# Three of the four weight sums of a Strassen group as accumulating loads instead of VectorE operations

## What is computed

```python
# block 1
h = rmsnorm(x, norm_ffn[l])
x = x + (jax.nn.silu(h @ w_gate[l]) * (h @ w_up[l])) @ w_down[l]
# block 2: a three-tap causal convolution along the tokens lies between
h2 = rmsnorm_2(x, ffn_norm_w[l])
up = causal_dwconv(h2 @ w_ffn_up[l], conv_w[l], conv_b[l])
a, b = jnp.split(up, 2, axis=-1)
x = x + (jax.nn.silu(a) * b) @ w_ffn_down[l]
```

## Time and profile before

| what | value |
|---|---|
| time, median of 3 runs | 2568.08 us (2567.1 to 2568.77) |
| profiled execution: its own time | 2568.49 us |
| its span in the trace | 2566.5 us |
| PE busy | 2531.9 us, 99% of the span, 11526 matmuls |
| DVE busy | 1851.5 us, 72% |
| ACT busy | 1300.8 us, 51% |
| POOL busy | 6.2 us |
| HBM read | 476.57 MB, 187 GB/s over the span |

### The profile page before, as it was taken

One profiled execution on the slowest core, in us unless ns is written; L12 is line 12 of the kernel. 1 busy time (PEld: TensorE's weight loads), 2 busy tenths in 40 slices (PEclk: granted clock), 3 DMA queues, 4 the chain that ended last, 5 costly groups with the idle time before them and its releaser, 6 DMA issues.

```text
span 2566.5 us, 28192 instructions
## 1 busy us (share of the span) xinstructions
PE 2531.9 (99%) x11526; PEld 2091.9 (82%) x11526; DVE 1851.5 (72%) x1646; ACT 1300.8 (51%) x1240; POOL 6.2 (0%) x15
## 2 busy tenths in 40 slices
PE   8999999999999999999999999999999999999997
PEld 7888888788888888888888888888888888888886
DVE  5565667788888888867554555555789999999996
ACT  6544555444444444455444553334565555555554
POOL 0000000000000000000000000000000000000000
PEclk9999999999999999999999999999999999999999
DMA  8455446655555555556555555556565555555551
GB/s 279 154 174 187 141 148 213 205 195 196 195 196 196 196 197 197 180 179 207 172 172 174 187 166 196 188 189 197 168 225 197 193 193 193 194 196 197 197 195 67
DMA packets 239616, 480.50 MB, mean 187 GB/s; under 512 B 7633, under 2 KB 7761, under 8 KB 239233
## 3 DMA queue, kind: packets, MB, share of 16 engines
q1 hardware_dynamic: 238496, 474.10, 55.2%
q0 software_dynamic: 992, 4.60, 0.5%
HBM read 476.57 MB, written 2.10 MB: 187 GB/s over the span
## 4 chain that ended last, share of the span: by engine, by line
PE 93%; DVE 3%; ACT 2%; issue 1%; DMA 0%; SPq 0%; DVEq 0%; ACTq 0%
PE acc L604 24%; PE acc L608 23%; PE acc L606 23%; PE misc L604 6%; PE misc L608 6%; PE misc L606 6%; PE misc L637 2%; ACT w_hi L1006 2%; DVE x L1459 1%; DVE w_lo L1431 1%; DVE hid L1791 0%; PE misc L721 0%; PE misc L701 0%; DMA x<-in_x 0%; PE misc L715 0%
## 5 line engine op out<-in xcount | busy, mean ns | idle before, releaser
L1431 DVE TENSOR_TENSOR w_lo<-w_raw,w_hi 128x2048 fp32r<-128x2048 f32 x407 | 930.6, 2290 | 361.9 <-ACT w_hi L1006 360.2
L1006 ACT ACTIVATE w_hi<-w_raw 128x2048 fp32r<-128x2048 f32 x407 | 778.8, 1916 | 501.6 <-PE acc L608 376.5
L604 PE MATMUL acc<-w_hi,xt_hi 128*128 128x512 f32 x1456 | 576.2, 396 | 0.4 <-issue 0.4
L608 PE MATMUL acc<-w_hi,xt_lo 128*128 128x512 f32 x1456 | 567.5, 390 | 0.0
L606 PE MATMUL acc<-w_lo,xt_hi 128*128 128x512 f32 x1456 | 566.7, 389 | 0.0
L604 PEld LDWEIGHTS acc<-w_hi,xt_hi 128*128 128x128 f32 x1456 | 273.6, 188 | 59.4 <-DVE x L1459 2.6
L608 PEld LDWEIGHTS acc<-w_hi,xt_lo 128*128 128x128 f32 x1456 | 273.3, 188 | 57.9
L606 PEld LDWEIGHTS acc<-w_lo,xt_hi 128*128 128x128 f32 x1456 | 273.6, 188 | 55.1
L1431 DVE TENSOR_TENSOR w_lo<-w_raw_more,w_hi 128x2048 fp32r<-128x2048 f32 x101 | 231.4, 2291 | 76.8 <-ACT w_hi L1006 76.5
L1006 ACT ACTIVATE w_hi<-w_raw_more 128x2048 fp32r<-128x2048 f32 x101 | 193.6, 1917 | 145.7 <-PE acc L608 79.4
L604 PE MATMUL misc<-w_hi,xt_hi 128*128 128x512 f32 x640 | 251.2, 393 | 3.6 <-DVE ht_lo L1437 3.6
(11 more groups left out here) (264 smaller groups left out, 3086.0 us busy)
## 6 DMA issues: line engine op xcount, KB each, us to landing
w_raw<-in_w_in SPq DMA_DIRECT2D x136, 1024.0 KB, 5.1
w_raw<-in_w_ffn_up SPq DMA_DIRECT2D x60, 1024.0 KB, 5.1
w_raw<-in_w_out SPq DMA_DIRECT2D x32, 1024.0 KB, 5.1
w_raw<-in_w_up SPq DMA_DIRECT2D x32, 1024.0 KB, 5.2
w_raw<-in_w_down SPq DMA_DIRECT2D x30, 1024.0 KB, 6.1
w_raw<-in_w_gate SPq DMA_DIRECT2D x28, 1024.0 KB, 5.2
w_raw_more<-in_w_ffn_up SPq DMA_DIRECT2D x28, 1024.0 KB, 5.0
w_raw<-in_w_ffn_down SPq DMA_DIRECT2D x28, 1024.0 KB, 7.0
```

What stands on the lines that cost most here:

```text
L604: nc.tensor.matmul(bank, hi[:, j, :], w_hi[:, t % RING, j, :], start=first and j == 0, stop=False, skip_group_check=shared)
L608: end = nc.tensor.matmul(bank, lo[:, j, :], w_hi[:, t % RING, j, :], start=False, stop=last and j == C - 1, skip_group_check=shared)
L1006: nc.scalar.activation(w_hi[:, t % RING], raw_tile(steps[t].slot), ACT.Copy).then_inc(hi_ready, 1)
L1431: nc.vector.tensor_tensor(w_lo[:, t % RING], raw_tile(steps[t].slot), w_hi[:, t % RING].bitcast(F32), ALU.subtract).then_inc(lo_ready, 1)
```

## The change

The sums for P7, P6 and P4 are no longer DVE operations. POOL issues for each a DMA that reads a weight tile from HBM and adds it to the raw slot in place (`accum_op=ALU.add`). The sum for P5 remains a DVE operation. Where the DVE operation subtracted, all four sums are now additions: T(P5) = B11 + B12, T(P7) = B12 + B22, T(P6) = T(P5) + B22, T(P4) = T(P6) + B21; the signs of the activation sums and of three result additions are turned to match. The tiles B22 and B21 are still loaded on their own for P3 and P2, so they are read from HBM twice or three times (B22 for P3, P7 and P6; B21 for P2 and P4).

POOL issues three such DMAs in each iteration, in this order: P7's after DVE's P5 sum, P6's after the `w_lo` of P5 is done, P4's after the `w_lo` of P6 is done (`lo_ready`). Each sum kind has a semaphore of its own, for which ACT waits before its `w_hi`. The slot of B22 is released once the `w_lo` of P3 is done (before: of U3, the step ahead of P7); the release of B21 comes to the same as before. The first hunk of the diff adds two blank lines only and is left out.

```diff
--- before.py
+++ after.py
@@ -111,7 +113,7 @@
 
 Load = namedtuple("Load", "weight row col slot release")
 Step = namedtuple("Step", "slot count")
-Sum = namedtuple("Sum", "count slot other other_count")
+Sum = namedtuple("Sum", "kind count slot other other_count weight row col ready")
 
 
 def plan_weights():
@@ -148,8 +150,8 @@
                  "G2": (a_weight, 2 * N, a_col), "G3": (a_weight, 3 * N, a_col),
                  "U2": (b_weight, 2 * N, b_col), "U3": (b_weight, 3 * N, b_col)}
         where.update({f"D{n}": (up_weight, (i - 1) * N, n * N) for n in range(Q)})
-        release = {"B11": at["P4"], "B12": at["P7"], "B22": max(at["P3"], at["P6"] - 1, at["P7"] - 1),
-                   "B21": max(at["P2"], at["P4"] - 1)}
+        release = {"B11": at["P4"], "B12": at["P7"], "B22": at["P3"],
+                   "B21": at["P2"]}
         here = {}
 
         def need(name):
@@ -159,8 +161,14 @@
 
         for name in order:
             if name in T_FORMS:
-                mine, other = need(T_FORMS[name][0]), need(T_FORMS[name][1])
-                sums[at[name]] = Sum(len(sums) + 1, mine.slot, other.slot, other.count)
+                mine = need(T_FORMS[name][0])
+                chunk = len(sums) // 4 + 1
+                if name == "P5":
+                    other = need("B12")
+                    sums[at[name]] = Sum(name, chunk, mine.slot, other.slot, other.count, None, None, None, None)
+                else:
+                    ready = {"P6": at["P5"], "P4": at["P6"], "P7": None}[name]
+                    sums[at[name]] = Sum(name, 16 * chunk, mine.slot, None, None, *where[T_FORMS[name][1]], ready)
                 steps.append(Step(mine.slot, None))
             else:
                 steps.append(need(RAW_FORMS.get(name, name)))
@@ -490,7 +498,7 @@
     dve_link = sem("dve_link")
 
     hid_ready = sem("hid_ready")
-    sum_ready = sem("weight_sum_ready")
+    sum_ready = {"P5": sem("t1_ready"), "P6": sem("t2_ready"), "P7": sem("t3_ready"), "P4": sem("t4_ready")}
     s_sum_ready = sem("s_sum_ready")
     s_hi_done = sem("s_hi_done")
     s_lo_done = sem("s_lo_done")
@@ -583,13 +591,28 @@
         load(mult_a[:], ins["mult_a"], tables_loaded)
         load(taps[:], ins["taps"], tables_loaded)
 
+        def weight_sums(ffn, i):
+
+            for name in ("P7", "P6", "P4"):
+                sm = sums[iteration_t(ffn, i) + order_of(ffn, i).index(name)]
+                if name == "P7":
+                    pool.wait_ge(sum_ready["P5"], nth(ffn, i))
+                else:
+                    pool.wait_ge(lo_ready, sm.ready + 1)
+                pool.dma_start(raw_tile(sm.slot), tile_of(ins[sm.weight][0], sm.row, sm.col),
+                               accum_op=ALU.add).then_inc(sum_ready[name], 16)
+
         pool.wait_ge(tile_used, FFN1_T + 1)
         load(final_row[:], ins["norm_final"].partition_broadcast(P), row_loaded)
+        for i in range(1, NF):
+            weight_sums(1, i)
         pool.wait_ge(lo_ready, more_free[1] + 1)
         load(decay[:], ins["decay"], tables2_loaded)
         load(rope_r[:], ins["rope_r"], tables2_loaded)
         load(causal[:], ins["causal"], tables2_loaded)
 
+        for i in range(1, NF):
+            weight_sums(2, i)
         pool.wait_ge(tile_used, iteration_t(2, NF - 1) + order_of(2, NF - 1).index("P4") + 1)
         load(final_row[:], ins["final_norm_w_2"].partition_broadcast(P), row_loaded)
 
@@ -998,7 +1021,7 @@
             if t >= STEPS:
                 return
             if t in sums:
-                act.wait_ge(sum_ready, sums[t].count)
+                act.wait_ge(sum_ready[sums[t].kind], sums[t].count)
             else:
                 act.wait_ge(raw_ready[steps[t].slot], steps[t].count)
             if t >= RING:
@@ -1413,16 +1436,16 @@
             links[0] += 1
             dve.wait_ge(dve_link, links[0])
 
-        def weight_sum(t):
+        def t1_sum(t):
 
             dve.wait_ge(raw_ready[sums[t].other], sums[t].other_count)
             mine = raw_tile(sums[t].slot)
-            nc.vector.tensor_tensor(mine, raw_tile(sums[t].other), mine, ALU.subtract).then_inc(sum_ready, 1)
+            nc.vector.tensor_tensor(mine, mine, raw_tile(sums[t].other), ALU.add).then_inc(sum_ready["P5"], 1)
 
         def split(t):
 
-            if t + 1 in sums:
-                weight_sum(t + 1)
+            if t + 1 in sums and sums[t + 1].kind == "P5":
+                t1_sum(t + 1)
             if t >= STEPS:
                 return
             if t not in sums:
@@ -1743,10 +1766,10 @@
                                          ALU.add))
             a11, a12, a21, a22 = (a_sum[:, k * C:(k + 1) * C, tok * P:(tok + 1) * P]
                                   for tok in range(TOK) for k in range(2))
+            link(nc.vector.tensor_tensor(s_sum[:, 0], a21, a22, ALU.subtract))
+            link(nc.vector.tensor_tensor(s_sum[:, 1], s_sum[:, 0], a11, ALU.subtract))
             nc.vector.tensor_tensor(s_sum[:, 2], a11, a21, ALU.subtract)
-            link(nc.vector.tensor_tensor(s_sum[:, 0], a21, a22, ALU.add))
-            link(nc.vector.tensor_tensor(s_sum[:, 1], s_sum[:, 0], a11, ALU.subtract))
-            nc.vector.tensor_tensor(s_sum[:, 3], a12, s_sum[:, 1], ALU.subtract).then_inc(s_sum_ready, 1)
+            nc.vector.tensor_tensor(s_sum[:, 3], a12, s_sum[:, 1], ALU.add).then_inc(s_sum_ready, 1)
 
         def s_lo_piece(ffn, lo, hi):
             dve.wait_ge(s_hi_done, ffn)
@@ -1758,23 +1781,23 @@
             scale = rstd[:, 1 if ffn == 1 else 4, :]
             key = (f"sums{ffn}", i)
 
-            def plus(dst, bank, tok):
+            def plus(dst, bank, tok, op=ALU.add):
                 return nc.vector.scalar_tensor_tensor(out=dst, in0=bank, scalar=scale[:, tok:tok + 1], in1=dst,
-                                                      op0=ALU.mult, op1=ALU.add)
+                                                      op0=ALU.mult, op1=op)
 
             if name == "P6":
                 dve.wait_ge(p5_copied, n)
                 dve.wait_ge(tile_used, t + 1)
-                plus(dst_b[:, 0, :], acc[:, 0, 0, :], 0).then_inc(p6_added, 1)
+                plus(dst_b[:, 0, :], acc[:, 0, 0, :], 0, ALU.subtract).then_inc(p6_added, 1)
             if name == "U3":
                 dve.wait_ge(p6_added, n)
                 dve.wait_ge(tile_used, t + 1)
-                plus(dst_b[:, 0, :], misc[:, 2, :], 0).then_inc(drained[2], 1)
+                plus(dst_b[:, 0, :], misc[:, 2, :], 0, ALU.subtract).then_inc(drained[2], 1)
             if name == "P7":
                 dve.wait_ge(p7_copied, n)
                 dve.wait_ge(tile_used, t + 1)
                 nc.vector.scalar_tensor_tensor(out=dst_b[:, 1, :], in0=acc[:, 0, 1, :], scalar=scale[:, 1:2],
-                                               in1=dst_a[:, 1, :], op0=ALU.mult, op1=ALU.add).then_inc(pair_read[0], 1)
+                                               in1=dst_a[:, 1, :], op0=ALU.mult, op1=ALU.subtract).then_inc(pair_read[0], 1)
             if name == "P2":
                 dve.wait_ge(p1_copied, n)
                 dve.wait_ge(tile_used, t + 1)
```

## The result

The changed kernel takes 2662.98 us (median of 4, 2659.81 to 2667.53), the kernel before on the same chip 2567.59 us (2565.57 to 2568.77). The ratio is 1.0378, with a 95% interval of 1.0365 to 1.0391: 95 us slower. The forecast was 2599 us, with a range up to 2650. (One of the four executions of e7 further down took 12046 us, for a reason that no run shows; its median counts that one, its ratio leaves it out.)

A forecast was written before the change was run, and what follows sets the result against it. The prediction took TensorE (PE) to bound the kernel nearly everywhere: nine second-stage stalls of 3.4 us, 31 us, on the profiled 2568.5 us gave 2599.5, less 0.4 for the median: 2599 us, range 2565 to 2650.

The forecast's parts named there:

- PE bounds the kernel, and the removed sums hide behind it: Whole kernel: PE busy 2531.9 of 2566.5 us; removing 60 sums, 137 us of DVE time, priced at nothing for PE.
- Throughput is no bound, only the latency of P6's DMA counts: Added DMAs: three add at most 15.6 us to 37.6 us of 64.8 per iteration; P6's has the least room.
- The free time is 7.9 us in the second stage and 10.8 in the first: Longest X before PE waits ahead of U2: 7.9 us in the second feed-forward stage, 10.8 in the first.
- X: Time from the end of P5's `w_lo` to P6's sum being ready; forecast 11.4 us in the second stage.
- X = 11.4 us: Second stage: P6's DMA queues behind P7's, shares with G3's and B21's loads, and lands at 2217.3, counted from 2205.94.
- 5.2 us in the sum: Engine time of one accumulating 1 MB DMA, taken as twice a plain load's 2.6 us.
- The factor of 1.5 for sharing: Accumulating DMA beside plain loads gets two thirds of the engines, so P6's 5.2 us become 7.8 us.
- the start of 1.9 us: Time from a DMA's issue to its first data, taken as about 1.9 us from plain loads.
- In the first stage it fits by 0.1 us: First stage: P6's sum lands at 738.9 against a limit of 738.8, 0.1 us, counted as nothing.
- The fall of the clock is left out of the forecast: Lower PE clock behind each second-stage stall: 15 to 21 us in nine iterations, kept only in the range.
- The sum was 31 us: Total forecast loss: PE idle 3.4 us ahead of U2 in nine second-stage iterations, nothing in the first stage.
- 6 us of stall, with a fallen clock: Second stage: the case that set the range's upper end, 2650 us.

The follow-up runs named there:

- e7: Changed kernel with the old release of B22's slot, at U3's `w_lo`, so G3's, B21's and D0's loads come later again: 2586.80 us, ratio 1.0074.
- e6: Changed kernel with P6's DMA issued ahead of P7's and ACT's copy of P5's result ahead of P6's `w_hi`: 2568.47 us, ratio 1.0002.
- e1: Changed kernel with P6's sum back on DVE; P7's and P4's stay accumulating DMAs: 2568.91 us, ratio 1.0005.
- e2: Changed kernel with POOL issuing P6's DMA ahead of P7's: 2578.94 us, ratio 1.0044.
- e4: Changed kernel with P6's DMA a plain copy without the addition, so P6 and P4 products differ from the reference: 2586.85 us, ratio 1.0072.
- e8: Changed kernel with P7's sum back on DVE and the old release of B22 that it needs: 2584.00 us, ratio 1.0069.

## Why the prediction was wrong

- *PE bounds the kernel, and the removed sums hide behind it*: right. e6 measures it: ratio 1.0002 with all of them gone.
- *Throughput is no bound, only the latency of P6's DMA counts*: right (e1, and e6 with all 60 DMAs).
- *The free time is 7.9 us in the second stage and 10.8 in the first*: right. The prediction counts X from the end of P5's `w_lo`, 0.3 us ahead of the issue. Counted so, the means less 7.9 give stalls of 5.8, 1.3, 1.9, 1.8 and 1.7 us, where 5.8, 1.4, 1.9, 1.9 and 1.8 were measured (changed kernel, e2, e4, e7, e8). The first stage has 13.1 - 10.8 = 2.3, measured 2.5.
- *X = 11.4 us*: this step failed; counted the same way 13.7 were measured in the mean and 13.9 in the iteration above. There, P6's packets were to begin 3.0 us after `w_lo` and began after 4.9, they were to take 7.8 us and took 8.7, and the landing took 0.3 instead of 0.6. The term that was too small is the time of one accumulating DMA's packets: 5.2 us in the sum, 6.0 us for the one alone (e2). It counts twice, since P7's DMA is drawn out by it too (7.4 us instead of 6.7). The 5.2 are twice a load at "some 400 GB/s", while the row named beside it, 329 GB/s at a share of 0.90, makes 366 GB/s at full share and twice 2.9 us. The rest of the late start is 0.8 us between P7's last packet and P6's first, in which G3's load moves alone; the sum has nothing there, and why it is so no run shows. The factor of 1.5 for sharing was about right (8.7 / 6.0 = 1.45), and so was the start of 1.9 us (2.0).
- The prediction overlooked that a third load, D0's, moves into the same stretch. The trace gives no sign that it counts: the other queue moves 131 GB/s beside P6's DMA whatever stands in it, and at that rate B21's load alone would last about 8 us (an estimate), past the end of P6's. No run takes D0's load away by itself.
- *In the first stage it fits by 0.1 us*: failed with the same X, 13.1 us instead of 10.9. The stall is 2.5 us nine times, 22 us.
- *The fall of the clock is left out of the forecast*: failed. The rows shown pointed at it for waits of 3.3 us and more; at 5.8 us it falls in every iteration (behind the shorter stalls of the first stage in three of nine), and over both stages it costs about 25 us, a quarter of the loss.
- The sum was 31 us and became 52 + 22 + 25 = 99 us in the profiled execution (95 us between the medians). The mechanism, the place and the count (nine, ahead of U2) were as written; of the 68 us too few, 2.3 us in one latency made 21 (second stage) and 22 (first stage), and the clock 25.

The range reached to 2650 us for "6 us of stall, with a fallen clock" in the second stage, and forgot that an X that long stalls the first stage as well.

The Trainium skill's rule that an add in the DMA path costs two source reads and runs at half the rate of a copy ("Collectives: The Full Stack", the bandwidth ceiling) agrees with this case: 207 GB/s against 398 in the windows above. The Trainium skill's 2.0 us plus bytes at 436 GB/s for a DMA issued by GpSimd ("DMA: Bandwidth & Descriptors", Anatomy of one DMA) comes to an estimated 4.4 us and does not hold for an accumulating one; 8.6 us is the shortest that the iterations shown here have.

## What to carry to other kernels

An engine with a high busy share is worth relieving only if the profile shows something that waits for it. Here DVE was 91% busy in a stage and its relief is worth nothing; two lines moved in its stream give 9 us.

Work moved to a DMA trades a duration for a latency. Before such a change, work out from the in-order stream of each engine what is queued behind the first instruction that waits for it. One small copy behind such a wait was worth 80 us, and it could have stood ahead.

A changed release of one buffer moves the loads of the next ones as well. Follow the whole chain of slots, and add what lands in the stretch in which the late transfer runs.

## What the runs showed of the hardware that I had not expected

- POOL is held 1.27 us by the issue of an accumulating DMA of 1 MB (512 rows of 2 KB), 0.78 us by that of a plain one of 1 MB (e4), and 0.54 us by its table loads, among them one of 1 MB in 128 packets of 8 KB.
- An accumulating DMA of 1 MB alone takes 8.6 us from issue to landing (the iteration of e2 above), a plain one 5.0. Its packets take 6.0 us of that, at 102 GB/s in the first us and at 209 GB/s from the third on.
- Beside each other the accumulating and the plain queue move the same bytes (131 GB/s each), so a plain load beside an accumulating DMA runs at a third of the 398 GB/s that it has alone.
- A plain load issued 2.9 us after e2's DMA for P6 moved no packet until that one was nearly through, and landed after 13.7 us instead of 5.1. What holds it back no run shows.
- The cost of an accumulating DMA is not additive with its company: 8.9 us in the mean ahead of P7's DMA (e2), 9.4 without the early loads (e7), 13.3 behind P7's and with the early loads.
